# A hybrid decoder step: the feed-forward and projection stages cut into five groups of 416 tokens, with four split-weight buffers

## The reference, cut to what is touched

```python
p = jnp.einsum('btd,de->bte', h, w_in_l)          # 1024 -> 3072, for prompt and sample tokens

def conv_ffn(h, conv_prev, w_gate_l, w_up_l, w_conv_l, b_conv_l, w_down_l):   # D_FF = 2816
    g = jnp.einsum('btd,df->btf', h, w_gate_l)
    u = jnp.einsum('btd,df->btf', h, w_up_l)
    gp = jnp.concatenate([conv_prev.astype(g.dtype), g], axis=1)
    gc = sum(gp[:, j:j + t_] * w_conv_l[j] for j in range(CONV_W)) + b_conv_l
    a = (jax.nn.gelu(gc.astype(jnp.float32)) * u.astype(jnp.float32)).astype(h.dtype)
    return jnp.einsum('btf,fd->btd', a, w_down_l), gp[:, -(CONV_W - 1):]
# x += rms_norm(conv_ffn(rms_norm(x)));  the last two gate rows are returned as the conv state
```

## Time and profile before

| | |
|---|---|
| median of 3 runs | 3869.59 us (3869.57 to 3871.64) |
| the profiled execution | 3877.51 us, of which the span 3875.7 us |
| TensorE busy | 3413.7 us (88%), mean granted clock 0.941 |
| DVE, ACT, POOL busy | 1787.7 (46%), 1279.2 (33%), 499.8 us (13%) |
| HBM read, written | 458 MB, 170 MB |
| projection | 66.6 to 708.9 us |
| feed-forward | 2145.1 us to the end |

### The profile page before, as it was taken

One profiled execution on the slowest core, in us unless ns is written; L12 is line 12 of the kernel. 1 busy time (PEld: TensorE's weight loads), 2 busy tenths in 40 slices (PEclk: granted clock), 3 DMA queues, 4 the chain that ended last, 5 costly groups with the idle time before them and its releaser, 6 DMA issues. The chain is left out here.

```text
span 3875.7 us, 55497 instructions
## 1 busy us (share of the span) xinstructions
PE 3413.7 (88%) x18718; PEld 2830.1 (73%) x18718; DVE 1787.7 (46%) x4203; ACT 1279.2 (33%) x2638; POOL 499.8 (13%) x395
## 2 busy tenths in 40 slices
PE   6999999598869994877699699999999999999994
PEld 5888888477769993443587587878787878788883
DVE  5112221267748782322497355255525542555322
ACT  4111111277757772322244222232223222322111
POOL 0000000144420001332253000010001000100001
PEclk7999999799989997989699799999999999999997
DMA  3433333634436556998376565346535653344221
GB/s 122 110 93 98 103 103 94 159 85 93 92 86 163 146 140 182 305 321 243 133 236 201 156 192 180 116 146 195 189 94 157 192 181 97 114 146 146 80 71 50
DMA packets 569941, 562.91 MB, mean 145 GB/s; under 512 B 42857, under 2 KB 467906, under 8 KB 564610
## 3 DMA queue, kind: packets, MB, share of 16 engines
q1 hardware_dynamic: 538484, 426.64, 39.5%
q0 software_dynamic: 19680, 65.42, 5.3%
q10 hardware_dynamic: 11600, 68.63, 5.2%
HBM read 458.15 MB, written 169.68 MB: 162 GB/s over the span
## 5 line engine op out<-in xcount | busy, mean ns | idle before, releaser
L2279 DVE TENSOR_TENSOR ff_wl<-ff_wr,ff_wh 128x1024 fp32r<-128x1024 f32 (+2 forms) x304 | 333.4, 1097 | 703.0 <-ACT ff_wh L2190 703.0
L2190 ACT ACTIVATE ff_wh<-ff_wr 128x1024 fp32r<-128x1024 f32 (+2 forms) x304 | 287.2, 945 | 911.6 <-PE ff_d L2113 300.7
L426 PE MATMUL pj_acc<-hT_h,pj_wh 128*128 128x512 f32 (+1 forms) x960 | 355.8, 371 | 11.0 <-POOL pj_wl L344 10.7
L426 PE MATMUL pj_acc<-hT_l,pj_wh 128*128 128x512 f32 (+1 forms) x960 | 326.7, 367 | 0.0
L2111 PE MATMUL ff_g<-ff_hh,ff_wh 128*128 128x512 f32 x704 | 295.5, 420 | 34.9 <-issue 15.1
L2111 PE MATMUL ff_d<-ff_ah,ff_wh 128*128 128x512 f32 x704 | 295.8, 420 | 16.8 <-DVE ff_al L2322 11.9
L2111 PE MATMUL ff_u<-ff_hh,ff_wh 128*128 128x512 f32 x704 | 289.8, 412 | 0.0
L2112 PE MATMUL ff_g<-ff_hh,ff_wh 128*128 128x512 f32 x704 | 278.8, 396 | 0.0
L2113 PE MATMUL ff_g<-ff_hh,ff_wl 128*128 128x512 f32 x704 | 277.6, 394 | 0.0
L2112 PE MATMUL ff_d<-ff_al,ff_wh 128*128 128x512 f32 x704 | 277.5, 394 | 0.0
L2113 PE MATMUL ff_d<-ff_ah,ff_wl 128*128 128x512 f32 x704 | 277.2, 394 | 0.0
(11 more groups left out here) (279 smaller groups left out, 6831.9 us busy)
## 6 DMA issues: line engine op xcount, KB each, us to landing
ff_wr<-in_w_gate SPq DMA_DIRECT2D x88, 512.0 KB, 3.8
ff_wr<-in_w_up SPq DMA_DIRECT2D x88, 512.0 KB, 5.1
sa_vca<-in_cache_a_v POOLq DMA_DIRECT2D x128, 256.0 KB, 8.3
sa_kca<-in_cache_a_k SPq DMA_DIRECT2D x128, 256.0 KB, 14.2
out<-in_cache_win_k ACTq DMA_DIRECT2D x64, 511.0 KB, 4.2
out<-in_cache_win_v ACTq DMA_DIRECT2D x64, 511.0 KB, 4.0
ff_wr<-in_w_down SPq DMA_DIRECT2D x64, 384.0 KB, 3.2
ff_wr<-in_w_down SPq DMA_DIRECT2D x64, 320.0 KB, 2.9
```

The costliest lines, as they stand in the source:

```text
L426: m = pe.matmul(acc[g][:, 0:width(g)], weights[:, k, c], part[:, c, cols], start=start, stop=stop)
L2190: act.activation(wh[:, slot % 2, 0:size], wr[:, slot, 0:size], ACT.Copy).then_inc(w_hi, 1)
L2279: dve.tensor_tensor(wl[:, slot % 2, 0:size], wr[:, slot, 0:size], wh[:, slot % 2, 0:size].bitcast(F32), ALU.subtract).then_inc(w_lo, 1)
```

## The change

**project:** five equal groups of 416 tokens (`PG`); the 32 samples are the last columns of the fifth. The halves become (0,1,2) and (3,4). q and k are split in five pieces a unit (the fifth has 384 columns). The turning of rows keeps its blocks of 512 and waits for the group that covers them.

**ffn:** five equal groups of 416 tokens (`NF`, `FG`), the samples being the last 32 of the fifth, in the same matmuls; the sample tiles and their operations go. `wh` and `wl` get four buffers, so that a cast waits only for unit n - 4. The down projection waits for `al` piece by piece. The last `turn_back` of a group comes after the next group's first gate product. Squares are taken per output tile beside the down projection (`squares`), sums by one reduce and one root over all rows, and the norms one per tile over the first four tiles. `xt` has two buffers. Constants go on ACT's queue and the hidden tile is loaded in two halves, the first after the first gate weights. In the last group the conv state is turned in six steps between down tiles (`turn_state`, `keep_state`) into a tile of its own. At the end DVE adds the residual for row blocks 2 and 3, loaded early into the free `hh`, and SP stores all blocks.

```diff
+PG = TOK // NAT
@@ project
-    SPLIT = [NAT * u + g for u in range(NU) if PROJ[u][1] != "v" for g in range(NG)]
+    SPLIT = [NAT * u + g for u in range(NU) if PROJ[u][1] != "v" for g in range(NAT)]
...
-                            cols = slice(g * GRP, g * GRP + width(g))
+                            cols = slice(g * PG, (g + 1) * PG)
...
-                pe.wait_ge(ev, raised(NAT * (NU * j + u) + g + 1 + NAT))
+                pe.wait_ge(ev, raised(NAT * (NU * j + u) + covering(g) + 1 + NAT))
...
-                    products(n, u, (0, 1))
+                    products(n, u, (0, 1, 2))
...
-                    products(n, u, (2, 3, 4))
+                    products(n, u, (3, 4))
@@ ffn
+NF = 5
+FG = TOK // NF
+FB = (FG + P - 1) // P
+FP = SEQ - (NF - 1) * FG
...
-        wh = s.sb("wh", [P, 2, DC, P], F32R)
-        wl = s.sb("wl", [P, 2, DC, P], F32R)
+        wh = s.sb("wh", [P, SLOTS, DC, P], F32R)
+        wl = s.sb("wl", [P, SLOTS, DC, P], F32R)
...
-        s.credit(mm, 2)
+        s.credit(mm, SLOTS)
@@ SP
                 load_w(n, 2 * k, wg_view[:, :, ds(f * P, P)])
+                if first:
+                    load_hidden(0, 0)
                 load_w(n + 1, 2 * k + 1, wu_view[:, :, ds(f * P, P)])
+                if first:
+                    load_hidden(0, 1)
...
-            def load_h(g):
+            def load_next(g, last):
-                sp.wait_ge(mm, raised(UNITS * g + 2 * FT + 2))
+                sp.wait_ge(mm, raised(UNITS * g + 2 * FT + SLOTS))
...
+                    for half in range(2):
+                        load_hidden(g + 1, half)
@@ TensorE
                 for c in range(size):
-                    a, b = first and c == 0, final and c == size - 1
-                    pe.matmul(dst[:], wh[:, k, c], src[0][:, c0 + c], start=a, stop=False)
-                    pe.matmul(dst[:], wh[:, k, c], src[1][:, c0 + c], start=False, stop=False)
-                    m = pe.matmul(dst[:], wl[:, k, c], src[0][:, c0 + c], start=False, stop=b)
-                    if last:
...
+                    half_in(c)
+                    pe.matmul(dst[:, 0:FG], wh[:, k, c], src[0][:, c0 + c], start=first and c == 0, stop=False)
+                    pe.matmul(dst[:, 0:FG], wh[:, k, c], src[1][:, c0 + c], start=False, stop=False)
+                    m = pe.matmul(dst[:, 0:FG], wl[:, k, c], src[0][:, c0 + c], start=False, stop=final and c == size - 1)
...
-                products(n, 0, gp[k], 0, DC, (hh[:, 0], hh[:, 1]), tp[0], hs, True, True, last)
+                products(2 * k, gp[k], 0, DC, (hh[:, 0], hh[:, 1]), True, True, half_in)
+                if first and isinstance(g, int) and g == 0:
+                    prepare()
+                elif first:
+                    turn_back(g - 1, DC - 1, 1)
...
-                pe.wait_ge(a_lo, raised(FT * (g + 1)))
                 pe.wait_ge(d_read, raised(DC * g + d + 1))
...
                 for j, size in enumerate(D_PARTS):
+                    c0 = sum(D_PARTS[:j])
+                    pe.wait_ge(a_lo, raised(FT * g + c0 + size))
                     pe.wait_ge(w_lo, raised(n + j + 1 + SLOTS))
...
+                if last and 1 <= d < 1 + (FT + 3) // 4:
+                    turn_state(d - 1)
@@ ACT
+            def squares(g, d):
+                act.wait_ge(y_ok, raised(DC * g + d + 1 + 2))
+                act.wait_ge(y_sum, raised(g))
+                act.wait_ge(y_sq, raised(DC * g + d))
+                for b in range(FB):
+                    r = rows_of(b)
+                    m = act.activation(junk[0:r, b], yn[0:r, b, ds(d * P, P)], ACT.Square, accum_out=s4[0:r, b, ds(d, 1)])
+                m.then_inc(y_sq, 1)
...
+                act.activation(yT[:], dp[k][:, 0:FG], ACT.Copy).then_inc(d_read, 1)
+                if not (isinstance(d, int) and d == 0):
+                    squares(g, d - 1)
@@ DVE
+            def beside(g, f):
+                if f == 0:
+                    dve.wait_ge(y_sq, raised(DC * (g + 1)))
+                    dve.tensor_reduce(s4[:, :, DC], s4[:, :, 0:DC], AX.X, ALU.add).then_inc(y_sum, 1)
+                    dve.wait_ge(y_sd, raised(g + 1))
+                    dve.reciprocal(s4[:, :, DC + 2], s4[:, :, DC + 1]).then_inc(y_rs, 1)
...
+                r = rows_of(f)
+                dve.scalar_tensor_tensor(yn[0:r, f], yn[0:r, f], s4[0:r, f, DC + 2:DC + 3], gain[0:r], ALU.mult,
+                                         ALU.mult).then_inc(y_norm, 1)
```

More of the change, by code:

```diff
@@ L425, in products @@
                                 stop = c == DC - 1 and weights is wl
-                                m = pe.matmul(acc[g][:, 0:width(g)], weights[:, k, c], part[:, c, cols],
+                                m = pe.matmul(acc[g][:, 0:PG], weights[:, k, c], part[:, c, cols],
                                               start=start, stop=stop)
@@ L1986, in rest @@
                         f_tile(g, 2 * i + k, k, DC, last)
-                        within(g, i, k)
+                        if not last:
+                            within(g, i, k)
                 f_tile(g, FT - 2, 0, DC, last)
@@ L2000, in groups @@
             head(0, False)
-            with eng.Fori(0, NG - 2) as g:
+            with eng.Fori(0, NF - 2) as g:
                 rest(g, False)
                 head(g + 1, False)
-            rest(NG - 2, False)
-            head(NG - 1, True)
-            rest(NG - 1, True)
-            for f in range(HEAD):
-                beside(NG - 1, f, True)
+            rest(NF - 2, False)
+            head(NF - 1, True)
+            rest(NF - 1, True)
         @block.sync
@@ new lines, in prepare, with products @@
+            def prepare():
+                pe.wait_ge(const_in, raised(16 * 4))
+                pe.transpose(tp[0][:, 0:(TAPS + 1) * FT], taps[:],
+                             ident[0:(TAPS + 1) * FT, 0:(TAPS + 1) * FT]).then_inc(pre_t, 1)
+                for f in range(FT):
+                    m = pe.transpose(tp[1][:, f * 16:f * 16 + 16], state[0:2 * DEC_B, f * P:(f + 1) * P], ident[0:16, 0:16])
+                m.then_inc(pre_t, 1)
+            def products(k, dst, c0, size, src, first, final, half_in=lambda c: None):
+                for c in range(size):
+                    half_in(c)
+                    pe.matmul(dst[:, 0:FG], wh[:, k, c], src[0][:, c0 + c], start=first and c == 0, stop=False)
+                    pe.matmul(dst[:, 0:FG], wh[:, k, c], src[1][:, c0 + c], start=False, stop=False)
+                    m = pe.matmul(dst[:, 0:FG], wl[:, k, c], src[0][:, c0 + c], start=False, stop=final and c == size - 1)
@@ new lines, in turn_back, with turn_state @@
+                m.then_inc(y_turned, 1)
+            def turn_state(m):
+                if m == 0:
+                    pe.wait_ge(g_read, raised(2 + FT * NF))
+                    pe.wait_ge(a_ok, raised(2 + FT * NF))
+                if m >= 2:
+                    pe.wait_ge(fin_r, raised(m - 1))
+                bank = (gp, up)[m % 2]
+                for f in range(4 * m, min(4 * m + 4, FT)):
+                    c = slice((f % 4) * P, (f % 4 + 1) * P)
+                    pe.transpose(bank[0][0:2, c], carry[:, f], ident[:])
+                    last = pe.transpose(bank[1][0:2 * DEC_B, c], tail[:, f].rearrange("p b j -> p (b j)"), ident[:])
+                last.then_inc(fin_t, 1)
@@ new lines, in f_tile @@
+                m.then_inc(conv2, 1)
+                dve.wait_ge(conv2, raised(q + 1))
+                for src, part in spans:
+                    m = dve.scalar_tensor_tensor(part(ca), src(2), tap(2, f), part(cb), ALU.mult, ALU.add)
+                m.then_inc(conv_ok, 1)
+                if last:
+                    dve.tensor_copy(tail[:, ds(f, 1)].rearrange("p o b j -> p (o b) j"), gs[:, k, :, DEC_T:])
+                dve.tensor_copy(carry[:, ds(f, 1), :].rearrange("p o j -> p (o j)"), gb[:, k, w:w + 2]).then_inc(carried, 1)
@@ L2371, in _ @@
[L2371 to L2380 removed]
+                if not (isinstance(d, int) and d == DC - 1):
+                    keep_turned(g, d, k)
@@ L2382, in program @@
+            groups(dve, f_tile, d_tile, beside, lambda g, last: None)
+            keep_turned(NF - 1, DC - 1, 1)
+            for b in range(FB):
+                beside(NF - 1, b)
+            dve.wait_ge(end_in, raised(32))
+            for b in (2, 3):
+                r = rows_of(b)
+                dve.wait_ge(y_norm, raised(FB * (NF - 1) + b + 1))
+                dve.tensor_tensor(yn[0:r, b], yn[0:r, b], x_end[b - 2][0:r].bitcast(F32), ALU.add).then_inc(end_in, 1)
 def program(nc, a, out):
```

438 lines of the change are left out of this document (176 added, 262 removed).

## The result

The changed kernel takes **3678.9 us** (median of 4 runs, 3675.7 to 3693.3) beside 3870.0 for the kernel before: a ratio of 0.9513, 95% interval 0.9488 to 0.9538. The forecast was 3623 us, so the sign was right and the time lies 56 us above it, and above the top of the range. The profiled execution is one of 3675.67 us with a span of 3674.1.

The account below looks back on a forecast made before the run. TensorE was taken to bound the kernel through matmul pace, holes and the feed-forward stage's two ends. Gains of 58 (projection), 134.6 (long stretch), 9 (start) and 45 (end) sum to 246.6 us, giving 3623 us; range 3592 to 3674.

Parts of the forecast that it names:

- Price of a 416-column matmul: TensorE matmuls: cost proportional to columns, 0.1842 us in feed-forward, 0.1871 in the projection.
- The other bound, 0.1867: Matmul price as streaming at 2.4 GHz plus a fixed part: 0.1867 us in feed-forward, 0.1903 in the projection.
- Projection: Projection stage: 120 matmuls of 416 columns a unit replace 96 wide and 24 narrow; gain 58 us.
- Waits for ff_al: Start of the down projection: waiting only for the tiles each piece reads removes the three 4-us waits and their cold clocks.
- Next late is the weight for the second output tile: Down projection: weights queued behind the next hidden group make TensorE wait 1.3 us, four times.
- Seams: Between feed-forward groups: DVE's norm, weight split and POOL overlap delay TensorE about 4 us a seam, four seams.
- rival 2: Seams stay late, slow clock returns: 60 us of waits, not 21; 3662 us. Sign: 10 us a seam for ff_wl. Chance 0.20.
- Four buffers: Feed-forward weights: four split buffers only add slack, nothing on the path in a steady tile.
- rival 1: Fixed part in each matmul, 0.1867 us (0.1903 in projection): +19.7 and +9.5 us, 3652 us. Chance 0.20.
- Start and end: Feed-forward stage's ends: start gains 9 us (5 to 13), end gains 45 us (42 to 47).
- Rival 3: Weight loads set the pace; a 416-column matmul costs as much as a 512-column one: 4083 us. Chance with rival 4 0.02.
- rival 4: Clock falls to 1.2 GHz with narrow matmuls, 0.347 us or more each: about 5360 us. Chance with rival 3 0.02.

Follow-up runs that it names:

- proj_only: Kernel before with only the projection's half of the change: 3819.0 us, ratio 0.9855 to the kernel before.
- hidden_late_1: Changed kernel, but SP issues the next group's hidden loads after the second down tile's weight loads instead of before: 3677.3 us, ratio 0.9490 to the kernel before.
- again_1: Changed kernel unedited, run again as yardstick: 3684.7 us, ratio 0.9508 to the kernel before.
- again_2: Changed kernel unedited, a second yardstick run: 3684.4 us, ratio 0.9518 to the kernel before.
- coarse_al: Changed kernel, but every down tile waits for all 22 ff_al tiles of its group, as before: 3689.4 us, ratio 0.9530 to the kernel before.
- the width run: Changed kernel with feed-forward matmuls narrowed to 384 (gate), 320 (up) and 256 (down) columns, sums incomplete: 3444.8 us.
- ffn_only: Kernel before with only the feed-forward half of the change: 3740.2 us, ratio 0.9662 to the kernel before.

## Why the prediction was right and wrong

The profiled execution came out at 3675.7, not 3631: 44.7 us. By the trace they are 52.7 in the long stretch, 3.2 in the projection and 0.6 at the end, less the 11.7 of the middle, which no one could forecast. The median missed by 56, 11 more, because I carried over that the profiled execution lay 8 us above the median; the one after lies 3 below.

- **Price of a 416-column matmul: wrong, the largest term.** 0.1878 against 0.1842 is 3.6 ns, and times 7896 it is 28.4 us; at the 0.1889 of most gate and up tiles it is some 4 more. The reading that failed is the earlier trace rows. Starts have two decimals, so the difference of two pairs is known to 5 ns a matmul or so. 0.0575 and 0.055 us for 128 columns cannot tell 0.0567 (proportional) from 0.0533 (2.4 GHz and a fixed part). Besides, a pair of 512 took 0.545 us, more than 2 x 0.2266, so it held another constant, which I did not subtract. The other bound, 0.1867, was nearly right, and I gave it 0.20. It deserved the larger share: in the earlier trace rows the 512-column step already lies 13.3 ns above its 213.3 ns of streaming.
- **Projection: right in its mechanism,** 54.8 of 58 us, the rest being the same price. proj_only shows the half alone: 588 us.
- **Waits for ff_al: right.** They are gone. "Next late is the weight for the second output tile" named the right place. It was priced at 1.3 us four times, measured 9.4 us in 4. SP stands at its wait for the last up product and puts four loads ahead of the weights; the cast began 12.97 us after that product (2298.9 to 2311.87), where I had the landing at 10.7. hidden_late_1 shows it by removal.
- **Seams: right mechanism, nearly right size.** 16 us were forecast, 20.6 measured. I took the stretch of the earlier trace rows for a norm's; it fell on a 2-column copy instead, with the same effect. The sign of rival 2, 10 us a seam, did not appear: it was 5.
- **Slow clock after holes: a term left at nothing.** The kernel before had 21 us of it by my own count, and my sum after had none, though it left 21 us of waits; rival 2 had it for holes of 3 us and more, but the stop of 2.44 us above was enough. The trace after shows 3 us of it, again_1 9, again_2 under 2, coarse_al 12. Some 3 us more went with the stops beyond what the list counts.
- **Transposes:** 204 at 0.13 rather than 0.11, 3.5 us.
- **Four buffers: right in steady tiles,** about 6 us of waits at the seams.
- **Slips that changed little.** 24 x 2.48 for the projection is 59.5, not 58, and 50 by the fixed form, not 48; rival 1's term there is 9.2, not 9.5. The conv state goes out in six steps, not seven. Of the stretch 1150 to 1350 us only the second half has a granted clock of 1.00; the first has 0.96, and with it 0.98 for the whole.
- **Start and end: right,** 24.7 (24.5) and 19.8 (19.2). Inside the end the four norms took 9.04 us rather than 7.2, since two of them were held by POOL's additions, and other steps were shorter.
- **Rivals.** Rival 1 came true (+29 us), and rival 2 in part: of its 39 us, some 16 are there, 9.6 of waits beyond the 21 forecast, 3 of clock and 3 to 4 that go with the stops. The price in both stages (28.4 + 4 + 3.2), these 16, and 4 for transposes and end lead from 3623 to 3679. That this meets the median is in part luck: the 11 us between profile and median and the 11.7 of the middle, which has nothing to do with the change, cancel. Rival 3 is out by the width run, rival 4 by a granted clock of 1.00 on the stretch. The range failed because its top took in rivals 1 and 2 one at a time. They are independent, 29 and 39 us above the forecast; and nothing was added for the variation between executions.

## What to carry to other kernels

Where thousands of equal instructions carry the sum, a price from a handful of rows with two decimals is not good enough: here 3.6 ns were 28 us in one stage. Take it from a long run of the same instruction, write it as columns over the clock plus a constant, and let the widest bound weigh as much as the nearest row. Rivals that can both be true must be added for the top of a range, and a wait that remains can bring slow clock with it, here 2 to 9 us from one execution to the next. Before giving POOL work to relieve DVE, look for what DVE does at the same time: moving the additions back to DVE, into a gap where it waited for ScalarE, took 21 us off, though DVE had more to do.

## What was not expected of the hardware

- A DVE copy of 2 columns took 2.36 us beside POOL's addition of 1024 columns, 1.27 beside one of 512, 0.16 without.
- TensorE's step per matmul was 12.2 to 15.7 ns above columns / 2.4 GHz at 256, 320, 384, 416 and 512 columns, while on the low clock 416 columns started every 0.346 us (8 steps from 2314.28 to 2317.05), which is columns / 1.2 GHz with nothing on top. What the 12 to 16 ns are was not tried.
- Stops of TensorE of 2 to 3 us were enough, not each time, for some 10 matmuls at 1.2 GHz (2313.76 to 2317.05 us). The same kernel had two such windows in its feed-forward stretch in one execution and six in another, whose stage was 7 us longer.
- The same code of the middle took between 1403 and 1418 us from one profiled execution to the next, with 11 to 31 us of waits for the cached keys (sa_kcb) among it. These waits alone do not explain it: ffn_only had 31.0 us of them in a short middle of 1404.9.
